# A four-layer decoder step with two recurrences: one recurrence narrowed to 320 columns, the state updates of the other stacked

## The reference

```python
def rglru_mixer(x, conv_state, h0, w_in, ...):        # layers 0 and 3
    u, gate = jnp.split(x @ w_in, 2, axis=-1)
    u, new_conv = causal_conv(u, conv_state, conv_w, conv_b)      # 4 taps
    r = sigmoid(blocks(u) @ w_a + b_a); i = sigmoid(blocks(u) @ w_x + b_x)
    log_a = -LRU_C * r * softplus(-lam)
    a = exp(log_a); b = sqrt(-expm1(2.0 * log_a)) * (i * u)
    b[:, 0] += a[:, 0] * h0
    h = linear_scan(a, b)                              # h_t = a_t h_{t-1} + b_t
    return (h * silu(gate)) @ w_out, new_conv, h[:, -1]

def hgrn2_mixer(x, s0, lb, w_in, norm_g, w_out):       # layer 2, 16 heads of 128
    q, f, v, gate = jnp.split(x @ w_in, 4, axis=-1)
    forget = lb + (1.0 - lb) * sigmoid(f); k = (1.0 - lb) * sigmoid(-f)
    o, s_new = gla_chunked(silu(q), k, v, log(forget), s0)
    ...
# in gla_chunked, per chunk (a sample's 8 tokens are one):
    S = S * exp(g_last)[..., None] + einsum('bshd,bshv->bhdv', k * exp(g_last - G), v)
```

## Time and profile before

| | |
|---|---|
| median of 3 runs | 2144.67 us (2142.47 to 2145.44) |
| the profiled execution | 2145.3 us |
| its span, first to last instruction | 2143.4 us |
| TensorE busy | 2010.6 us (94%) |
| VectorE busy | 1242.6 us (58%) |
| ScalarE busy | 905.9 us (42%) |
| GpSimd busy | 994.8 us (46%) |
| granted TensorE clock, mean | 0.963 |

### The profile page before, as it was taken

The page is one execution under the profiler, slowest core; times in us unless marked ns, Lnnn a source line. Parts: engine busy times, 40 slices in busy tenths (PEclk is TensorE's granted clock), DMA queues, the critical chain, the costliest instruction groups (busy, mean ns, idle before and its releaser), DMA issues.

```text
span 2143.4 us, 35491 instructions
## 1 busy us (share of the span) xinstructions
PE 2010.6 (94%) x13874; PEld 1788.5 (83%) x13874; DVE 1242.6 (58%) x2220; ACT 905.9 (42%) x1501; POOL 994.8 (46%) x1245
## 2 busy tenths in 40 slices
PE   5898999998999999999999999998999999989987
PEld 4887989698888898897898888887898888879966
DVE  6688442426787777744256566666354147873443
ACT  3476522333544444333353343333242347663332
POOL 4667705036445554150365455555432347665602
PEclk8999999999999999999999999999899999999997
DMA  4443466635434445475452344444386344435850
GB/s 126 132 136 125 133 214 229 213 99 163 117 109 132 134 133 153 161 256 189 131 169 75 112 130 125 135 136 135 103 289 205 135 147 132 142 119 168 280 203 25
DMA packets 331590, 324.36 MB, mean 151 GB/s; under 512 B 21560, under 2 KB 312288, under 8 KB 331424
## 3 DMA queue, kind: packets, MB, share of 16 engines
q1 hardware_dynamic: 330560, 321.75, 47.0%
q10 hardware_dynamic: 864, 0.34, 0.1%
HBM read 292.41 MB, written 29.61 MB: 150 GB/s over the span
## 4 chain that ended last, share of the span: by engine, by line
PE 63%; DVE 25%; ACT 5%; issue 3%; DMA 2%; SPq 1%; POOL 0%; ACTq 0%; DVEq 0%
PE ps L751 9%; PE ps L752 9%; PE ps L756 8%; PE ps L1361 5%; PE ps L1370 4%; DVE work L2288 3%; DVE work L2133 2%; PE ps L741 2%; DVE work L2418 2%; PE ps L1427 2%; PE ps L742 2%; PE ps L743 2%; PE ps L1168 2%; PE ps L1444 1%; PE ps L1474 1%
## 5 line engine op out<-in xcount | busy, mean ns | idle before, releaser
L1593 POOL TENSOR_TENSOR wl<-raw,wh 128x256 fp32r<-128x256 f32 x1216 | 990.3, 848 | 1115.1 <-ACT wh L1613 1114.7
L751 PE MATMUL ps<-Hh,wh 128*128 128x320 f32 x1280 | 400.2, 326 | 25.2 <-DVE Hl L2172 12.2
L1613 ACT ACTIVATE wh<-raw 128x1024 fp32r<-128x1024 f32 x304 | 311.8, 1053 | 193.4 <-PE ps L756 52.9
L752 PE MATMUL ps<-Hl,wh 128*128 128x320 f32 x1280 | 385.2, 314 | 0.0
L751 PEld LDWEIGHTS ps<-Hh,wh 128*128 128x128 f32 x1280 | 246.2, 192 | 48.5 <-issue 24.2
L752 PEld LDWEIGHTS ps<-Hl,wh 128*128 128x128 f32 x1280 | 246.7, 193 | 1.5
L2133 DVE TENSOR_SCALAR work<-ps 128x512 f32<-128x512 f32 (+9 forms) x236 | 108.1, 474 | 208.1 <-DMA out_rgh_s<-work 50.9
L756 PE MATMUL ps<-Hh,wl 128*128 128x320 f32 x1280 | 215.1, 310 | 0.0
L756 PEld LDWEIGHTS ps<-Hh,wl 128*128 128x128 f32 x1280 | 196.1, 189 | 0.0
L751 PE MATMUL ps<-Oh,wh 128*128 128x320 f32 x512 | 156.8, 318 | 3.7 <-DVE Ol L2859 3.7
L752 PE MATMUL ps<-Ol,wh 128*128 128x320 f32 x512 | 155.6, 316 | 0.0
(11 more groups left out here) (412 smaller groups left out, 3809.4 us busy)
## 6 DMA issues: line engine op xcount, KB each, us to landing
raw<-rg_w_in SPq DMA_DIRECT2D x128, 256.0 KB, 3.6
raw<-hg_w_in SPq DMA_DIRECT2D x128, 256.0 KB, 4.8
raw<-ssd_w_in SPq DMA_DIRECT2D x96, 256.0 KB, 4.0
work<-cache_mem_k SPq DMA_DIRECT2D x40, 512.0 KB, 6.0
raw<-rg_w_out SPq DMA_DIRECT2D x64, 256.0 KB, 3.5
raw<-x_w_k SPq DMA_DIRECT2D x64, 256.0 KB, 3.6
raw<-x_w_v SPq DMA_DIRECT2D x64, 256.0 KB, 3.5
raw<-x_w_q SPq DMA_DIRECT2D x64, 256.0 KB, 5.4
```

The lines of the kernel that those rows point to most:

```text
L751: pe.matmul(ps[:, bank, 0:n], high(half, k), mh[:, k, 0:n], start=(k == 0), stop=False)
L752: pe.matmul(ps[:, bank, 0:n], high(half, k), ml[:, k, 0:n], start=False, stop=False)
L1593: ins = pool.tensor_tensor(out, src, wh[:, parted(n) % HALVES, r:r + 2].bitcast(F32), ALU.subtract)
L1613: act.activation(wh[:, nx.n % HALVES], raw[:, slot, :, half * P:(half + 1) * P], ACT.Copy).then_inc(hi_ready, 1)
```

## The change

In the recurrence, tap 3 of the convolution writes the 256 prompt columns and the 64 sample columns of the result apart, into tiles of 320 columns; everything behind it (`take_ri`, the gates, `update`, `scan`, `product`) has 320 columns instead of 344, and `product` is one instruction instead of two. The taps 0 to 2 still run on 344, now in the one tile `rg_w`.

In HGRN2 the 64 rows of samples stand twice on the 128 partitions. Rows 64 to 127 of `hg_v[:, 2]` are copied by a DMA to rows 0 to 63; above stays v, below VectorE subtracts v's rounded part (`hg_vh`). The keys are transposed onto both halves (one transpose more a head) and split by VectorE into a rounded part and the rest (`hg_kp`). `gain` is then two matmuls of rounded float32 (fp32r) over 128 partitions, instead of one float32 matmul over 64. The PSUM of keys and values is released as soon as it is copied, and the splits come behind. The last update of a group, `gain(j,1,1)`, moves from behind `take_v(i,2)` to between the two units of the next `take_g`.

```diff
-        rg_in, rg_u = [c(2, EXT), c(2, EXT)], [c(2, EXT), c(2, EXT)]
-        rg_r, rg_i, rg_t, rg_a = c(2, EXT), c(2, EXT), c(2, EXT), c(2, EXT)
+        rg_in, rg_w, rg_u = [c(2, EXT), c(2, EXT)], c(2, EXT), [c(2, NT), c(2, NT)]
+        rg_r, rg_i, rg_t, rg_a = c(2, NT), c(2, NT), c(2, NT), c(2, NT)
...
-                                mm = pe.matmul(ps[:, 4 + 2 * m + j, 0:CV], w, rg_u[i % 2][:, k, 0:CV], start=(k == 0), stop=(k == 1))
+                                mm = pe.matmul(ps[:, 4 + 2 * m + j, 0:NT], w, rg_u[i % 2][:, k, :], start=(k == 0), stop=(k == 1))
...
                     project(gfv(i), 0)
+                    if i >= 2:
+                        gain(i - 2, 1, 1)
                     project(gfv(i) + 1, 1)
...
-                    pe.transpose(ps[:, 5, 256:384], hg_k[:, h, NT - P:NT], ident[:]).then_inc(S("hg_kt_full"), 1)
+                    pe.transpose(ps[:, 5, 256:384], hg_k[:, h, NT - P:NT], ident[:])
+                    pe.transpose(ps[0:64, 5, 256:384], hg_k[:, h, SEQ:NT], ident[:]).then_inc(S("hg_kt_full"), 1)
...
-                    v = hg_vm[64:P, 4 * half:4 * half + 4, :]
-                    pe.matmul(ps[:, 7, :], hg_kt[64:P, 2, :], v, start=True, stop=True).then_inc(S("hg_sn_full"), 1)
+                    if half == 0:
+                        pe.wait_ge(*past("hg_kp_ready", i * 2 + (h + 1)))
+                    v = hg_vm[:, 4 * half:4 * half + 4, :]
+                    pe.matmul(ps[:, 7, :], hg_kp[:, 0, :], v, start=True, stop=False)
+                    pe.matmul(ps[:, 7, :], hg_kp[:, 1, :], v, start=False, stop=True).then_inc(S("hg_sn_full"), 1)
...
                     take_v(i, 2)
-                    gain(j, 1, 1)
                     sums(j)
                 pe.wait_ge(*past("hg_q_read", GROUPS))
                 take_out()
+                gain(6, 1, 1)
                 take_out()
...
-                        steps.did(act.activation(rg_r[:, j, 0:CV], ps[:, 4 + j, 0:CV], ACT.Sigmoid, bias=column(1, j)))
+                        steps.did(act.activation(rg_r[:, j, 0:NT], ps[:, 4 + j, 0:NT], ACT.Sigmoid, bias=column(1, j)))
...
-                    act.activation(hg_v[:, 2, :], ps[:, a + 1, 0:256], ACT.Copy).then_inc(S("hg_v_read"), 1)
+                    act.activation(hg_v[64:P, 2, :], ps[64:P, a + 1, 0:256], ACT.Copy).then_inc(S("hg_v_read"), 1)
+                    act.wait_ge(*past("hg_v_read", i + 1))
+                    steps.did(act.activation(hg_vh[64:P], hg_v[64:P, 2, :], ACT.Copy))
+                    steps.sync()
+                    act.dma_start(hg_v[0:64, 2, :], hg_v[64:P, 2, :]).then_inc(S("hg_v_twice"), 16)
...
-                            ins = stt(u[:, j, 0:CV], own[:, j, k:k + CV], tap(k, j), u[:, j, 0:CV], MUL, ADD)
...
+                            did(stt(rg_w[:, j, 0:CV], own[:, j, k:k + CV], tap(k, j), rg_w[:, j, 0:CV], MUL, ADD))
+                    sync()
+                    for j in range(2):
+                        did(stt(u[:, j, 0:SEQ], own[:, j, 3:SC], tap(3, j), rg_w[:, j, 0:SEQ], MUL, ADD))
+                        ins = stt(u[:, j, SEQ:NT].rearrange("p (b s) -> p b s", b=NB), samples(own, SC)[:, j, :, 3:SEG], tap(3, j), samples(rg_w, SC)[:, j, :, 0:NL], MUL, ADD)
...
-                    did(tt(rg_o[:, :, 0:SEQ], rg_r[:, :, 0:SEQ], g[:, :, 0:SEQ], MUL))
-                    tt(by_seq(rg_o), apart(rg_r), by_seq(g), MUL).then_inc(S("rg_o_done"), 1)
+                    tt(rg_o, rg_r, g, MUL).then_inc(S("rg_o_done"), 1)
...
-                    copy(hg_kt, ps[:, 5, 0:384].rearrange("p (t c) -> p t c", t=3)).then_inc(S("hg_kt_read"), 1)
+                    did(copy(hg_kx, ps[:, 5, 256:384]))
+                    copy(hg_kt, ps[:, 5, 0:256].rearrange("p (t c) -> p t c", t=2)).then_inc(S("hg_kt_read"), 1)
+                    sync()
+                    did(copy(hg_kp[:, 0, :], hg_kx))
+                    sync()
+                    tt(hg_kp[:, 1, :], hg_kx, hg_kp[:, 0, :].bitcast(F32), SUB).then_inc(S("hg_kp_ready"), 1)
...
                     if h == 0:
-                        wait("hg_v_read", i + 1)
+                        wait("hg_v_twice", 16 * (i + 1))
+                        did(tt(hg_v[sm, 2, :], hg_v[sm, 2, :], hg_vh[sm].bitcast(F32), SUB))
+                        sync()
```

More of the change, by code:

```diff
@@ L199, in trunk @@
         gate_area = sb("gate_area", [P, 4 * (CV + 1)])
-        WORK = 15984
+        WORK = 16288
+        HG_PARTS = 7936
+        with ExitStack() as layout:
+            layout.enter_context(nc.sbuf_tensor("hg_below", [P, HG_PARTS], F32))
+            hg_vm, hg_kp = (layout.enter_context(nc.sbuf_tensor(name, [P, n, P], F32R)) for name, n in (("hg_vm", NB), ("hg_kp", 2)))
+            hg_vh = layout.enter_context(nc.sbuf_tensor("hg_vh", [P, 256], F32R))
         work = sb("work", [P, WORK])
@@ L1702, in gates @@
                     for j in range(2):
-                        steps.did(act.activation(rg_t[:, j, 0:CV], rg_r[:, j, 0:CV], ACT.Tanh, scale=column(4, j)))
+                        steps.did(act.activation(rg_t[:, j, 0:NT], rg_r[:, j, 0:NT], ACT.Tanh, scale=column(4, j)))
                     ahead(r0 + 2)
```

66 lines of the change are left out of this document (35 added, 31 removed).

## The result

The changed kernel takes 2155.2 us (median of 6 runs, 2150.55 to 2159.79) against 2143.1 us for the kernel before in the same comparison (6 runs, 2131.07 to 2145.44): ratio 1.0062, 95% interval 1.0036 to 1.0088. It is slower by some 12 us. The forecast was 2135, and the measured time lies above its range; the third rival, "the new wait lowers the clock", had 2152.

A forecast was written before the change was run, and what follows sets the result against it. TensorE was taken as the main bound (63% of the chain, VectorE 25%), its savings counting only where it does not await VectorE. Terms -6.7 - 1.8 - 2.7 + 1.7 = -9.5 us gave 2135 us, range 2122 to 2147.

The forecast's parts named there:

- the third rival: HGRN2 loop: new wait at turn_back(i,0) lowers the clock in most turns, GpSimd holds VectorE's added instructions; 2152 us, chance 0.09.
- The recurrence, -6.7: Recurrence, both layers: fewer columns and one product instruction save 3.4 us a layer, 6.7 us in two; bounds 2 and 10.
- The second rival: Recurrence gives nothing: tap 3's added instructions are held beside GpSimd, TensorE's saving vanishes in the gate's wait; 2141 us, chance 0.14.
- five VectorE-bound groups a layer: Recurrence: in five groups a layer VectorE is the bound, and its gain of 0.45 us each gives 2.3 us.
- HGRN2, ahead of turn_back(i,0): HGRN2 turn: VectorE's copy of keys comes 0.50 us later, the loop 0.19 us longer here, TensorE waits some 1.7 us.
- it does not matter: HGRN2 turn: TensorE reaches turn_back(i,0) 1.5 us earlier, without effect, as VectorE now sets this point.
- only get later (by 0.6): HGRN2 turn: ScalarE's weight rounding comes 0.6 us later, with four units in hand, and costs nothing.
- From there on, -0.45: HGRN2 turn behind turn_back(i,0): gain(i,0,0) saves 0.6 us, an added transpose costs 0.15, so 0.45 us less.
- The 1.28 us at `gain(j,1,0)`: HGRN2 turn: TensorE's wait of 1.28 us ahead of gain(j,1,0) stays, as VectorE's chain before it is untouched.
- The clock, +1.7: HGRN2 loop: one more stretch at half clock in seven turns, behind the new wait at turn_back(i,0), costs 1.7 us.
- since behind the unit its bank is free: HGRN2 turn: moving gain(j,1,1) between take_g's units removes its 0.60 us wait, counted in TensorE's 1.5 us earlier arrival.
- The tail, -2.7: HGRN2, updates of group 7: cheaper gains save 2.7 us after later keys and a transpose; range 1 to 3.

The follow-up runs named there:

- run 1: Only the recurrence's part of the change, on the kernel before, HGRN2 as before: 2139.2 us against 2141.4, ratio 0.998 (0.9957 to 1.0003).
- Run 6: The whole change, with ScalarE's first rounding of weights in a turn put behind its sigmoid of q: 2145.3 us, ratio 1.0001 to the kernel before.
- run 4: The whole change, but with gain(j,1,1) back behind take_v(i,2): 2128.0 us, ratio 0.9927 to the kernel before.
- run 5: The whole change plus one bare TensorE wait behind take_v(i,2) for VectorE's new_state(j,1,0), no work moved: 2125.3 us, ratio 0.9917 to the kernel before.
- run 13: The kernel before with gain(j,1,1) moved as in the change and one idle VectorE multiplication added a turn: 2153.7 us, ratio 1.0071.
- run 7: The change with VectorE's finish moved behind the scores and hg_q, and gain(j,1,1) back behind take_v(i,2): 2119.4 us, ratio 0.9891 to the kernel before.
- run 15: The kernel before, gain(j,1,1) in its old place, with two idle VectorE multiplications added a turn: 2158.3 us, ratio 1.0083.
- run 3: The whole change, with VectorE's finish(i-1) moved behind the scores and hg_q: 2112.9 us, ratio 0.9849 to the kernel before.

## Why the prediction was wrong

**The recurrence, -6.7: right in kind, too large.** Records of `take_ri` 4.56 us (forecast 4.55), late groups 20.18 (20.1), the gate's wait nearly gone. The profiles show -3.4 in layer 3, the forecast's figure for a layer, and -1.2 in layer 0; run 1's median shows 2.2. The traces of all runs settle it. From the first to the last `take_ri` layer 0 takes 148.2 to 149.3 us in the nine with the old recurrence and 146.8 to 147.8 in the eight with the new one, layer 3 137.1 to 138.6 and 133.7 to 136.2; the means differ by 1.4 and 3.5, together 4.9. The second rival, nothing gained, isn't excluded by the interval of run 1, but by these it is. The forecast counted five VectorE-bound groups a layer, though the earlier trace rows has six in both: four of layer 0's intervals were 20.6 to 20.7 us, two of layer 3's 20.6 and 21.1. In the sum this moves little.

**HGRN2, ahead of turn_back(i,0): the instructions right, what they meet left out.** VectorE was to be 0.50 us later; its own added work is 0.46 + 0.06. A gain is two records of 0.23 us, as forecast (1220.44, 1220.68, next matmul 1220.91); right behind a wait it takes 0.57 (1207.69 to 1208.26). The step that failed here is the sentence that TensorE arrives earlier and "it does not matter". It does: the keys of the first head come earlier too, ScalarE rounds weights and GpSimd splits them 2.33 us earlier (17.61 less 15.28), and `finish` is held for 1.77 us. The forecast had looked at ScalarE's work as something that could only get later (by 0.6). VectorE's part of the turn was to be 0.2 us longer and is 1.9 us longer in the turn read above (21.39 + 0.05 against 19.21 + 0.36); over seven turns that is 11.1 us instead of 1.3. Run 6 puts the price at about 2.6 us a turn, with what the clock adds. The Trainium skill (GPSIMD Engine Reference, section 1, Specifications) has contention for VectorE instructions with two SBUF inputs and for those in a 2-port mode. L2670 and L2676, with two inputs, agree (1.97 and 1.23 us instead of 1.01 and 0.82); the copy to `Oh` reads one and is held as well (0.90 instead of 0.49), and whether it runs in that mode no run here shows.

**From there on, -0.45: about right, not as derived.** With no lowered stretch ahead of the second head's scores, TensorE's piece is 31.0 us in runs 4 and 5 against 31.7: 0.7 less, 0.36 on TensorE up to these scores and 0.35 on VectorE behind them, which the forecast did not look at. The 1.28 us at `gain(j,1,0)`, which were to stay, are 0.60; as TensorE is off the piece there, this changes nothing in it. Run 4 is what the forecast had priced, but for the gain's place: turns of 51.1 us in three of its four (forecast 51.0), and 2128 us, inside the range.

**The clock, +1.7: the step that failed.** "I count one, in seven turns, because the periods shift against each other" was argued from nothing in the trace. The wait was 4.0 to 5.1 us instead of 1.7, and in the change a lowered stretch came with each of the six waits in the loop, 6.8 us long, and TensorE's piece behind them cost 2.6 to 4.0 us more than with the clock up (33.6 to 35.0 against 31.0). Over the seven turns TensorE's pieces grew by 13.9 us, where 0.7 less each (runs 4 and 5) would have made 5 less: 19 us for the clock instead of 1.7. These 17 us too little and the 10 of VectorE's part make 27; the smaller errors (the tail, the recurrence, the 0.45) and what the change does not touch bring that to the 24 between the profiles and the forecast. For the medians it is 20. Whether the forecast's own wait of 1.7 us would have lowered the clock behind `turn_back` stays open: in these turns 1.5 did not and 2.2 did. But run 13 shows that a turn with as little as 0.8 us more of delay does not stay at the one lowered stretch either: its seven turns take 12.9 us more than before, and the dose is 5.6 of them. The place of the gain was in the text as a gain, "since behind the unit its bank is free". With VectorE late it was a loss: the 0.6 us of wait that it removed, and what came on top as TensorE got faster, 3.05 us in run 4, had stood in front of sums and a projection unit, where the wait was mostly free. Of the ten waits of 3.0 to 3.1 us there or in the same place (runs 4, 5 and 7) four had a lowered stretch over or behind them, at some 1.6 us.

**The tail, -2.7: too small.** It was -6.8. Behind group 7's `turn_back`, in its steps, 15.6 us are lowered instead of 23.5, which is 4.0 us of TensorE; the rest is what was counted for the updates.

**The third rival** had the mechanism, lowered stretches at `turn_back(i,0)` and VectorE held by GpSimd, with 0.09. Its condition, two stretches in three turns, was met by far. It deserved more of the chance: that VectorE is busy up to 0.31 us before the point was read, and so was the lowered stretch behind `outputs(j,1)`, where 1.28 us of idle time stand ahead of small matmuls. The new place had a wait of about that size ahead of matmuls of the same kind. The rows alone did not decide it, as the 1.2 to 1.5 us of runs 13 and 15 show; that the wait would be 4 to 5 us followed from the hold of `finish`, which the rival had with 0.55 us instead of 1.8.

## What to carry to other kernels

Find the ring: which piece of which engine the turn consists of, and to which engine the spare time belongs. An edit that frees TensorE where VectorE sets the turn gives nothing, moves the spare time to one point, and advances every engine behind it, here GpSimd onto VectorE's last instructions. So first shorten the other engine's piece (an instruction whose result nobody awaits goes behind the one that is awaited, run 3), and only then free TensorE.

A wait has a place besides a length. Here 4.0 us of wait in one piece ahead of a run of small matmuls cost a stretch at half clock on the piece that sets the turn, every time; parted in 3.05 and 0.86, with the larger one ahead of sums and projection units and where TensorE had time to spare, they cost none in most turns. If time to spare is left over, put it where the engine has slack and large matmuls follow. And follow the chain across all engines: 12 of the 32 us of TensorE's piece are VectorE's and ScalarE's.
